# Giving the gathered expert tokens their own contiguous tiles in a two-layer diffusion step with mixture of experts

## The chip, the cores and the metric

The kernel runs on one core of a Trainium2 chip. The metric is the time of one execution on the device in microseconds, as the median of several runs. All weights come from HBM in fp32.

## The reference

Two groups of 128 tokens of width 1024 (a prompt and a sample) go through two layers. Layer 0 is latent attention beside a short convolution, then a dense SwiGLU of inner width 2816. Layer 1 is a convolution module, then a SwiGLU with 8 experts of inner width 3584, of which each token uses the two best. What matters here is the last part:

```python
logits = (t @ router).astype(jnp.float32)
top_v, top_i = lax.top_k(logits, TOP_K)          # TOP_K = 2, t is (256, 1024)
w = jax.nn.softmax(top_v, axis=-1)
gates = jnp.sum(jax.nn.one_hot(top_i, N_EXPERTS) * w[..., None], axis=-2)
for e in range(N_EXPERTS):                       # 8 experts
    out = out + gates[:, e:e + 1] * _swiglu(t, w_gu[e], w_down[e])
```

`_swiglu(h, w_gu, w_down)` is `(silu(h @ gate) * (h @ up)) @ w_down`.

## The kernel before

The program is written engine by engine, each engine with its own fixed list of instructions, and semaphores between them are placed by hand. Nothing derives a wait from the tiles that an instruction touches.

**The weight stream.** SyncE loads weights in pieces of 1 MB into the seven slots of `raw`. ScalarE copies a piece into `high` with the type fp32r (`part` in its `experts`, L763; L489 for the dense pieces), VectorE takes the difference `raw - high` into `low` (L1326), and TensorE multiplies with three products per tile (`mm3`, L1410 to L1412): high half of the tokens by `high`, high half by `low`, low half by `high`. The token tile, 128 x 128, is the stationary operand that is loaded as a weight, and 512 columns of the weight piece are the moving operand. A semaphore `piece_used` then lets SyncE fill the slot again.

**One expert.** Each of the 8 experts has 14 units. A unit is a gate-up product over 8 tiles of the inner dimension (24 matmuls, `gate_up`) into one bank, a Silu on ScalarE (L767), a product on VectorE (L1331), two transposes on TensorE (`e_T`, L1927), a split of the result into `upH` and `upL` (ScalarE L773, VectorE L1336) and a down product of 12 matmuls (`e_down`) that runs two units behind.

**The tokens of an expert.** `gather` (TensorE, L1899) picks up to 128 tokens out of `tokH` and `tokL` by 32 matmuls of 128 columns against `pickR`, in four groups of eight; each group fills one bank and raises `gathered`. `gather_out` (ScalarE, L749 to L755) copies the four banks, one ACTIVATE of 128 x 512 for each, into `slotH` and `slotL` and raises `slot_ready`. `slotH` and `slotL` are no tiles of their own: they are the first 128 of the 256 columns of each of the 8 rows of `hidH` and `hidL`, which hold the split activations of the dense layers and are free by then. `gate_up` reads them as `slotH[:, kk, :]` and `slotL[:, kk, :]`. The profile therefore calls them hidH and hidL.

**Order at the end of an expert.** TensorE transposes the last unit, gathers the tokens of the next expert, does the last two down products of this one, waits for four `slot_ready`, does the first gate-up product of the next expert, and scatters this expert's result (`backR` by `outH` and `outL`, L1969 and L1971). ScalarE does `act_high` of the last unit, the four copies of `gather_out`, three high copies of the weight stream, two copies into `outH` (L802), a further high copy and the next Silu. For expert 0 nothing stands between `gather(0)` and the wait for `slot_ready` but a wait for VectorE's output of a modulation gate (L901). A second pass over all experts is in the program for an expert with more than 128 tokens; it isn't taken here.

**Tiles.** `sb` takes tiles from a stack: those opened with `where=ph` are given back at `ph.close()`, and the next phase begins at the same address. The expert phase begins with `tokH` and `tokL` and goes on with `outH`, `outL`, `eact`, `pick`, `pickR`, `backR` and small tiles.

Of the kernel before, what the change touches and what calls it, by code (L numbers as in the profile page):

```python
# [16 lines left out]
F32R = mybir.dt.float32r  # L17
# [5 lines left out]
P = 128  # L23
D = 1024
KT = D // P
KH = KT // 2
# [105 lines left out]
def ahead(u):  # L132

    return 3 * u + 4 if u else LEAD
# [5 lines left out]
def build(nc, t, outs):  # L140
    ctx = ExitStack()
    with ctx:
        def sb(name, shape, dt=F32, where=None):
            return (where or ctx).enter_context(nc.sbuf_tensor(name, shape, dt))
# [9 lines left out]
        hidH = sb("hidH", [P, KT, TILES * P], F32R)  # L154
        hidL = sb("hidL", [P, KT, TILES * P], F32R)
        gate = sb("gate", [P, TILES, D])
        ph = ExitStack()
# [3 lines left out]
        ph = ExitStack()  # L161
# [14 lines left out]
        ph = ExitStack()  # L176
# [11 lines left out]
        ph = ExitStack()  # L188
        act = sb("act", [P, 2, TILES, UNIT], where=ph)
        ph.close()  # L190
        ph = ExitStack()
# [8 lines left out]
        ph = ExitStack()  # L200
        tokH = sb("tokH", [P, TILES, D], F32R, where=ph)
        tokL = sb("tokL", [P, TILES, D], F32R, where=ph)
        outH = sb("outH", [P, D], F32R, where=ph)
        outL = sb("outL", [P, D], F32R, where=ph)
        eact = sb("eact", [P, 2, UNIT], where=ph)
# [9 lines left out]
        bank = ctx.enter_context(nc.psum_tensor("bank", [P, 8, 512], F32))  # L215
# [11 lines left out]
        prob_l = work[:, HEADS * P:].rearrange("p (h n) -> p h n", h=HEADS)  # L227
        probT = hid[:, 0:4, :].rearrange("p k n -> p (k n)").rearrange("p (g m n) -> p g m n", g=2, m=4)
        rope_t = gate[:, 1, 0:HEADS * ROPE].rearrange("p (h d) -> p h d", h=HEADS)

        slotH, slotL = hidH[:, :, 0:P], hidL[:, :, 0:P]

        sems = {}

        def S(name):
            if name not in sems:
                sems[name] = ctx.enter_context(nc.semaphore(name))
            return sems[name]
# [15 lines left out]
        def cat(ap):  # L254
            return ap.rearrange("p a b -> p (a b)")
# [148 lines left out]
        def expert_value(first, i):  # L404

            slot = (first + i) % RAWS
            within = sum(16 if STREAM_E[m][0] == "d" else 32 for m in range(i + 1) if (first + m) % RAWS == slot)
            per = sum(16 if STREAM_E[m][0] == "d" else 32 for m in range(PER_E) if (first + m) % RAWS == slot)
            passes = (first - N_DENSE) // (EXPERTS * PER_E)
            return slot_total(slot) + passes * EXPERTS * per + within, per  # L410
# [42 lines left out]
        def _(a):  # L453
# [285 lines left out]
            def experts(first, split, passes):  # L739
                ge = passes * EXPERTS  # L740

                def picked(e):

                    a.wait_ge(S("pick_ready"), e + (ge + 1))
                    a.activation(pickR[:, :, :], pick[:, :, :], ACT.Copy).then_inc(S("pickR_ready"), 1)

                def gather_out(e):

                    for part, dst in enumerate((slotH, slotL)):  # L749
                        for kh in range(2):  # L750
                            i = 2 * part + kh
                            a.wait_ge(S("gathered"), e * 4 + (4 * ge + i + 1))
                            a.activation(dst[:, kh * KH:(kh + 1) * KH, :],
                                         bank[:, (6, 0)[part] + kh, :].rearrange("p (k n) -> p k n", k=KH),
                                         ACT.Copy).then_inc(S("slot_ready"), 1)  # L755

                def part(e, kind, u):
                    i = NUM_E[(kind, u)]
                    n, m = first + i, split + i
                    value, per = expert_value(first, i)  # L760
                    a.wait_ge(S(f"raw_in{n % RAWS}"), e * per + value)
                    a.wait_ge(S("piece_used"), e * PER_E + (m - SPLITS + 1))
                    a.activation(high[:, m % SPLITS, :], raw[:, n % RAWS, :], ACT.Copy).then_inc(S("high_ready"), 1)  # L763

                def silu(e, u):
                    a.wait_ge(S("piece_used"), e * PER_E + (split + NUM_E[("b", u)] + 1))
                    a.activation(eact[:, u % 2, :], bank[:, u % 2, 0:UNIT], ACT.Silu).then_inc(S("e_silu"), 1)  # L767

                def act_high(e, w):
                    a.wait_ge(S("e_T"), e * UNITS_E + (ge * UNITS_E + w + 1))  # L770
                    if w >= 2:
                        a.wait_ge(S("piece_used"), e * PER_E + (split + NUM_E[("d", w - 2)] + 1))
                    a.activation(upH[:, w % 2, :, 0:P], bank[:, 2 + w % 2, 0:UNIT].rearrange(  # L773
                        "p (c n) -> p c n", c=UC), ACT.Copy).then_inc(S("e_high"), 1)

                def parts(e, i0, i1, last=True):

                    for i in range(i0, i1):
                        if i < PER_E:
                            part(e, *STREAM_E[i])  # L780
                        elif not last:
                            part(e + 1, *STREAM_E[i - PER_E])

                def body(e, last):
                    for u in range(1, UNITS_E):
                        parts(e, ahead(u - 1), ahead(u), last)
                        silu(e, u)
                        act_high(e, u - 1)
                        if u == 5:
                            a.wait_ge(S("back_T"), e + (ge + 1))  # L790
                            a.activation(cat(backR[:, :, :]), bank[:, 6, 0:TILES * P], ACT.Copy).then_inc(
                                S("back_ready"), 1)
                        if u == 7 and not last:
                            picked(e + 1)
                    parts(e, ahead(UNITS_E - 1), PER_E + 2, last)
                    act_high(e, UNITS_E - 1)
                    if not last:
                        gather_out(e + 1)
                    parts(e, PER_E + 2, PER_E + LEAD - 1, last)
                    for h in range(2):  # L800
                        a.wait_ge(S("piece_used"), e * PER_E + (split + PER_E))
                        a.activation(outH[:, h * 512:(h + 1) * 512], bank[:, 4 + h, :], ACT.Copy).then_inc(  # L802
                            S("out_high"), 1)
                    if not last:
                        parts(e, PER_E + LEAD - 1, PER_E + LEAD, last)
                        silu(e + 1, 0)

                if passes:
                    parts(0, 0, LEAD)
                picked(0)  # L810
                gather_out(0)
                if not passes:
                    parts(0, 3, LEAD)
                silu(0, 0)
                with a.Fori(0, EXPERTS - 1) as e:
                    body(e, False)
                body(EXPERTS - 1, True)
# [1218 lines left out]
```

## Time and profile before

| | |
|---|---|
| median of three runs | 1692.38 us (1691.88 to 1696.34) |
| the profiled execution: its time, its span | 1696.34 us, 1694.6 us |
| instructions | 20850 |
| TensorE matmul busy, weight loads busy | 1532.0 us (90%), 1227.0 us (72%) |
| VectorE, ScalarE, GpSimd busy | 1225.2 us (72%), 975.4 us (58%), 18.6 us (1%) |
| mean granted TensorE clock, in parts of full speed | 0.949 |
| read from HBM | 469.75 MB |

Each engine has its own busy time; a group of instructions is named by the line of the program, the engine, the operation and the tiles, output first. Matmuls are pipelined, so that the duration of one (389 ns) is longer than the distance between the starts of two (0.23 us); the distance is what counts for the time. "PEld" is the loading of stationary operands, which overlaps the matmuls. The experts run from about 682 us to the end.

### The profile page before, as it was taken

To read this page: it belongs to the slowest core of one execution; us is meant where nothing else is said; L and a number is where in the kernel's file an instruction comes from. 1 tells how busy PE (TensorE), PEld (TensorE's weight loads), DVE (VectorE), ACT (ScalarE), POOL (GpSimd) and SP (SyncE) were. 2 spreads that over 40 slices of the span, in tenths; PEclk is the share of its full clock that TensorE was granted. 3 is DMA by queue.
4 is the path that set the end of the run, shared out by engine and by line. 5 is a ranking of instruction groups with operands and counts; after the bars stand their busy time and mean duration, and the time that the engine had idled before them with its cause. 6 is when DMAs were issued, how large, how long until landed. Compare 5 with 4: busy or idle time off the path is not lost.

```text
span 1694.6 us, 20850 instructions
## 1 busy us (share of the span) xinstructions
PE 1532.0 (90%) x7157; PEld 1227.0 (72%) x7157; DVE 1225.2 (72%) x1171; ACT 975.4 (58%) x978; POOL 18.6 (1%) x25
## 2 busy tenths in 40 slices
PE   3658878999788957999999999999999999999996
PEld 1536556888575746788888888888888888888885
DVE  0454555445458744888888988988988988888886
ACT  1231424434244643677777777677677777777773
POOL 0000000000000000000000000000000000000000
PEclk9878899999898978999999999999999999999998
DMA  8455684565535506799999999999999999999993
GB/s 302 171 210 182 213 276 148 188 194 180 173 124 174 199 6 218 241 366 367 326 367 365 331 366 346 354 367 345 353 367 348 353 366 345 355 366 335 353 367 127
DMA packets 340213, 471.64 MB, mean 278 GB/s; under 512 B 13023, under 2 KB 274861, under 8 KB 340158
## 3 DMA queue, kind: packets, MB, share of 16 engines
q1 hardware_dynamic: 336176, 464.43, 80.2%
q0 software_dynamic: 1216, 4.28, 0.7%
q10 hardware_dynamic: 2766, 2.22, 0.4%
q8 instruction: 32, 0.52, 0.1%
q14 instruction: 23, 0.19, 0.0%
HBM read 469.75 MB, written 1.13 MB: 278 GB/s over the span
## 4 chain that ended last, share of the span: by engine, by line
PE 82%; DVE 8%; DMA 3%; ACT 3%; issue 2%; POOL 0%; ACTq 0%; SPq 0%; DVEq 0%; POOLq 0%
PE bank L1410 23%; PE bank L1412 23%; PE bank L1411 23%; PE bank L1785 2%; PE bank L1422 2%; DMA raw<-moe_gu 2%; PE bank L1899 1%; DVE low L833 1%; PE bank L1927 1%; DVE hid L1178 1%; DMA x<-x_sample 1%; PE bank L1439 1%; PE bank L1458 1%; ACT high L489 1%; ACT high L763 1%
## 5 line engine op out<-in xcount | busy, mean ns | idle before, releaser
L1326 DVE TENSOR_TENSOR low<-raw,high 128x2048 fp32r<-128x2048 f32 x333 | 757.4, 2289 | 117.2 <-ACT high L763 109.4
L763 ACT ACTIVATE high<-raw 128x2048 fp32r<-128x2048 f32 x333 | 635.6, 1919 | 182.7 <-DMA raw<-moe_gu 114.0
L1410 PE MATMUL bank<-high,hidH 128*128 128x512 f32 (+1 forms) x1264 | 499.4, 395 | 35.8 <-DVE hidL L870 24.9
L1412 PE MATMUL bank<-high,hidL 128*128 128x512 f32 (+1 forms) x1264 | 495.1, 392 | 0.0
L1411 PE MATMUL bank<-low,hidH 128*128 128x512 f32 (+1 forms) x1264 | 495.1, 392 | 0.0
L1410 PEld LDWEIGHTS bank<-high,hidH 128*128 128x128 f32 x1264 | 239.9, 190 | 91.2 <-DVE hidL L870 28.0
L1412 PEld LDWEIGHTS bank<-high,hidL 128*128 128x128 f32 x1264 | 239.5, 189 | 50.2
L1411 PEld LDWEIGHTS bank<-low,hidH 128*128 128x128 f32 x1264 | 240.1, 190 | 48.9 <-issue 0.2
L1410 PE MATMUL bank<-high,upH 128*128 128x512 f32 (+1 forms) x550 | 227.4, 413 | 2.8 <-DVE upL L963 2.8
L1412 PE MATMUL bank<-high,upL 128*128 128x512 f32 (+1 forms) x550 | 216.9, 394 | 0.0
L1411 PE MATMUL bank<-low,upH 128*128 128x512 f32 (+1 forms) x550 | 215.7, 392 | 0.0
L833 DVE TENSOR_TENSOR low<-raw,high 128x2048 fp32r<-128x2048 f32 (+3 forms) x59 | 131.4, 2245 | 52.3 <-ACT high L489 52.1
L1412 PEld LDWEIGHTS bank<-high,upL 128*128 128x128 f32 x550 | 104.3, 190 | 23.8
L489 ACT ACTIVATE high<-raw 128x2048 fp32r<-128x2048 f32 (+3 forms) x59 | 109.2, 1884 | 18.9 <-DMA raw<-w_in 18.1
L1410 PEld LDWEIGHTS bank<-high,upH 128*128 128x128 f32 x550 | 104.6, 190 | 21.5 <-DVE upL L963 3.0
L1411 PEld LDWEIGHTS bank<-low,upH 128*128 128x128 f32 x550 | 105.0, 191 | 18.5
L767 ACT ACTIVATE eact<-bank 128x256 f32<-128x256 f32 x112 | 42.0, 375 | 61.3 <-PE bank L1412 60.9
L643 ACT ACTIVATE act<-bank 128x256 f32<-128x256 f32 x22 | 7.3, 381 | 109.3 <-PE bank L1412 109.3
L1127 DVE TENSOR_TENSOR act<-act,bank 128x256 f32<-128x256 f32 x22 | 8.3, 418 | 79.6 <-ACT act L643 79.6
L1178 DVE SCALAR_TENSOR_TENSOR hid<-uT,taps,hid 128x256 f32<-128x256 f32 x150 | 60.1, 477 | 0.1
L1422 PE MATMUL bank<-raw,cond 128*32 128x512 f32 x384 | 50.8, 654 | 8.2 <-DVE ada L881 7.8
L697 ACT ACTIVATE diag<-const,taps 128x128 f32<-128x128 f32 x93 | 36.5, 401 | 27.2 <-PE bank L1785 24.9
(222 smaller groups left out, 979.2 us busy)
## 6 DMA issues: line engine op xcount, KB each, us to landing
raw<-moe_gu SPq DMA_DIRECT2D x448, 512.0 KB, 5.4
raw<-moe_down SPq DMA_DIRECT2D x112, 1024.0 KB, 6.3
raw<-ada_w SPq DMA_DIRECT2D x48, 1024.0 KB, 6.1
raw<-ffn_gu SPq DMA_DIRECT2D x44, 512.0 KB, 4.8
raw<-ffn_down SPq DMA_DIRECT2D x11, 1024.0 KB, 4.9
raw<-conv_pw SPq DMA_DIRECT2D x16, 512.0 KB, 4.3
raw<-w_in SPq DMA_DIRECT2D x6, 1024.0 KB, 7.2
raw<-w_o SPq DMA_DIRECT2D x4, 1024.0 KB, 6.9
```

The lines of the kernel that those rows point to most:

```text
L489: a.activation(high[:, n % SPLITS, 0:w], raw[:, m % RAWS, 0:w], ACT.Copy).then_inc(S("high_ready"), 1)
L697: st.mark(a.activation(diag[:, i % DIAGS, :], ident, ACT.Copy, scale=taps[:, j * KT + k:j * KT + k + 1]), "diag_ready")
L763: a.activation(high[:, m % SPLITS, :], raw[:, n % RAWS, :], ACT.Copy).then_inc(S("high_ready"), 1)
L767: a.activation(eact[:, u % 2, :], bank[:, u % 2, 0:UNIT], ACT.Silu).then_inc(S("e_silu"), 1)
L833: v.tensor_tensor(low[:, STREAM[SPLIT[n]] % RAWS, 0:w], raw[:, STREAM[SPLIT[n]] % RAWS, 0:w], high[:, n % SPLITS, 0:w].bitcast(F32), ALU.s ...
L1178: st.mark(v.scalar_tensor_tensor(dst, src, w, dst, ALU.mult, ALU.add), "conv_part")
L1326: v.tensor_tensor(low[:, n % RAWS, :], raw[:, n % RAWS, :], high[:, m % SPLITS, :].bitcast(F32), ALU.subtract).then_inc(S("low_ready"), 1)
L1410: pe.matmul(out, xh, wh, start=start, stop=False)
L1411: pe.matmul(out, xh, wl, start=False, stop=False)
L1412: return pe.matmul(out, xl, wh, start=False, stop=stop)
L1422: last = pe.matmul(bank[32 * k:32 * k + 32, b, :], cond[:, kh * KH + k, :], w_slot(raw, m % RAWS, (KH, 512))[:, k, :], start=kh == 0, stop ...
L1785: st.mark(pe.matmul(bank[:, k % 2, 0:TILES * P].rearrange("p (t n) -> p t n", t=TILES), diag[:, i % DIAGS, :], uT[:, k, :, j:j + P], start ...
```

## The change

`slotH` and `slotL` become tiles of their own, each 128 partitions x 8 x 128 elements (4 KB in a partition), placed in the expert phase between `tokL` and `outH`, so that everything behind them in that phase moves up by 8 KB. The copy in `gather_out` writes 512 consecutive elements and reads a bank of 512 elements as one row, where it had four rows of 128 with a step of 256 elements on the writing side. Waits, semaphores, matmuls, DMAs and the order on each engine stay as they are.

```diff
         tokH = sb("tokH", [P, TILES, D], F32R, where=ph)
         tokL = sb("tokL", [P, TILES, D], F32R, where=ph)
+        slotH = sb("slotH", [P, KT, P], F32R, where=ph)
+        slotL = sb("slotL", [P, KT, P], F32R, where=ph)
         outH = sb("outH", [P, D], F32R, where=ph)
...
-
-        slotH, slotL = hidH[:, :, 0:P], hidL[:, :, 0:P]
...
                             a.wait_ge(S("gathered"), e * 4 + (4 * ge + i + 1))
-                            a.activation(dst[:, kh * KH:(kh + 1) * KH, :],
-                                         bank[:, (6, 0)[part] + kh, :].rearrange("p (k n) -> p k n", k=KH),
+                            a.activation(cat(dst[:, kh * KH:(kh + 1) * KH, :]), bank[:, (6, 0)[part] + kh, :],
                                          ACT.Copy).then_inc(S("slot_ready"), 1)
```

`cat(ap)` is `ap.rearrange("p a b -> p (a b)")`.

## Rows read from the trace of the kernel before

**Rows 1.** The page: its head, and the 40 slices of TensorE, clock and DMA.

```profile
span 1694.6 us, 20850 instructions
PE   3658878999788957999999999999999999999996
PEclk9878899999898978999999999999999999999998
DMA  8455684565535506799999999999999999999993
```

**Rows 2.** Windows of about one expert: span, busy time and count per engine, clock, DMA.

```profile
core 0: us, PE busy (x) PEld busy (x) DVE busy (x) ACT busy (x) POOL busy (x), PEclk, DMA share, GB/s
925.00:1050.00 125.00, 124.39 (x577) 102.49 (x576) 110.19 (x82) 93.03 (x79) 0.00 (x0) 1.00 1.03 354
1175.00:1300.00 125.00, 125.00 (x587) 103.32 (x586) 110.37 (x82) 92.75 (x80) 0.00 (x0) 1.00 1.04 355
```

**Rows 3.** Waits of TensorE's loads, 690 to 1660 us: total, times, longest.

```profile
PEld bank L1927 <- DVE eact L1331: 6.0, 7, 1.7
```

**Rows 4.** DMA from 700 to 1660 us: rates in 40 slices.

```profile
GB/s 364 367 368 375 312 346 366 364 377 315 341 367 368 367 327 346 367 363 367 368 307 366 368 367 368 309 367 363 366 374 300 367 367 368 374 304 343 364 368 373
```

**Rows 5.** Line 753, the copies of `gather_out`: duration min/median/max, first and last start.

```profile
L753 ACT ACTIVATE hidH<-bank x16: 597/597/599, 684.5 to 1550.0; 128x512 fp32r<-128x512 f32 x16
L753 ACT ACTIVATE hidL<-bank x16: 597/597/599, 686.3 to 1551.8; 128x512 fp32r<-128x512 f32 x16
```

**Rows 6.** Groups of ScalarE by shape: copies of 128 x 512 out of a bank.

```profile
L802 ACT ACTIVATE outH<-bank 128x512 fp32r<-128x512 f32 x16 | 8.6, 591 | 5.1 <-PE bank L1412 5.1
L651 ACT ACTIVATE upH<-bank 128x512 fp32r<-128x512 f32 x11 | 6.6, 598 | 3.4 <-PE bank L1704 3.4
L571 ACT ACTIVATE vals<-bank 128x512 f32<-128x512 f32 x3 | 1.7, 579 | 0.0
L618 ACT ACTIVATE hidH<-bank 128x512 fp32r<-128x512 f32 x2 | 1.2, 594 | 0.3 <-PE bank L1642 0.3
```

**Rows 7.** Timeline, end of the first expert, in order of time.

```profile
801.88 0.20 PEld L1927 LDWEIGHTS bank<-const,eact 128*128 128x128 f32 x2 [1.57 <-DVE eact L1331]
803.20 0.60 ACT L753 ACTIVATE hidH<-bank 128x512 fp32r<-128x512 f32 x1 [0.39 <-PE bank L1899]
805.88 0.60 ACT L753 ACTIVATE hidL<-bank 128x512 fp32r<-128x512 f32 x1 [0.30 <-PE bank L1899]
806.37 5.52 ACT L763 ACTIVATE high<-raw 128x2048 fp32r<-128x2048 f32 x3
808.32 6.70 DVE L1326 TENSOR_TENSOR low<-raw,high 128x2048 fp32r<-128x2048 f32 x3 [3.50 <-ACT high L763]
810.98 0.19 PEld L1410 LDWEIGHTS bank<-high,hidH 128*128 128x128 f32 x1
```

**Rows 8.** Timeline, start of the first expert.

```profile
685.77 1.42 DVE L901 TENSOR_TENSOR gate<-bank,gate 128x512 f32<-128x512 f32 x2
687.16 0.60 ACT L753 ACTIVATE hidL<-bank 128x512 fp32r<-128x512 f32 x1 [0.29 <-PE bank L1899]
687.83 0.19 PEld L1410 LDWEIGHTS bank<-high,hidH 128*128 128x128 f32 x1 [0.84 <-DVE gate L901]
```

**Rows 9.** Line 1410, 690 to 1660 us: duration min/median/max, first and last start.

```profile
L1410 PEld LDWEIGHTS bank<-high,hidH x884: 187/188/188, 690.5 to 1659.3; 128*128 128x128 f32 x177
L1410 PEld LDWEIGHTS bank<-high,upH x432: 187/188/192, 704.7 to 1653.9; 128*128 128x128 f32 x144
```

**Rows 10.** The tile hidH from 600 us on: matmuls that read it.

```profile
L1410 PE MATMUL bank<-high,hidH x928: 387/389/796, 625.9 to 1668.0; 128*128 128x512 f32 x186
```

**Rows 11.** Timeline of TensorE: ends of runs of down, gate-up and scatter products.

```profile
806.43 0.39 PE L1410 MATMUL bank<-high,upH 128*128 128x512 f32 x1
...
810.97 0.39 PE L1412 MATMUL bank<-high,upL 128*128 128x512 f32 x1
...
811.88 0.39 PE L1410 MATMUL bank<-high,hidH 128*128 128x512 f32 x1
...
816.41 0.39 PE L1412 MATMUL bank<-high,hidL 128*128 128x512 f32 x1
816.64 0.40 PE L1969 MATMUL bank<-outH,backR 128*128 128x512 f32 x1
818.27 0.39 PE L1971 MATMUL bank<-outL,backR 128*128 128x512 f32 x1
```

## Prediction

> **What bounds the kernel now.** I read the page first, then windows of one expert each, then the waits, and last the stretch around the changed copies. The page shows that TensorE is at nine tenths or more in every slice of the second half, where the experts run, with the clock at its upper level and the DMA engines equally full [rows 1]. The changed instructions run only there. The windows of an expert say the same more sharply: 124.4 and 125.0 us of matmul in 125 us at a granted clock of 1.00, with VectorE at 110 and ScalarE at 93 us [rows 2]. The matmul busy time is modelled, so I checked it by the waits: the loads of TensorE waited for another engine 6.0 us in 970, seven times, all of it for the last activation of an expert, one wait for each boundary between experts [rows 3].
>
> DMA is a close second. It moves 367 GB/s in most slices and falls to 304 to 315 in about one slice in four or five, at the boundaries [rows 4]. One expert needs 3 x 1024 x 3584 x 4 bytes = 44.04 MB, which at 367 GB/s takes 120.0 us. The distance between experts follows from the copies themselves: the first of the first expert starts at 684.5, the second of the eighth at 1550.0 [rows 5], so (1550.0 - 684.5 - 0.9) / 7 = 123.5 us, where 0.9 is the distance from one copy to the next ((805.88 - 803.20) / 3 [rows 7]). TensorE's own list gives that too: 504 matmuls of 512 columns at 0.2265 to 0.227 us (next part) are 114.2 us, and the remaining 9 are the gather, the scatter, the transposes and the wait. So TensorE's list sets the time of the experts, and if it got shorter, DMA would take over 3.5 us further down.
>
> **The copies.** The change touches 4 copies for each of 8 experts, 32 in all. Each takes 597 ns, with hardly a spread (597 to 599) [rows 5]. What would one of 512 consecutive elements take? The nearest rows are the copies of a whole bank of 128 x 512: into `outH`, consecutive and fp32r as the new one will be, 591 ns; into `vals`, 579 ns; into `upH`, a step between parts, 598 ns; and into the first layer's `hidH`, with the very step that the change removes, 594 ns [rows 6]. The stepped ones lie at 594 to 598, the consecutive ones at 579 to 591, so the step costs at most a few ns. I take 591, the row that agrees in type, shape and source, that is 6 ns less. The bounds are 579 (18 ns less) and 598 (1 ns more). In work this is 32 x 6 ns = 0.19 us, at most 0.58 us, of an engine that has about 30 us free in each 125.
>
> The Trainium skill puts a number on such a copy, in "ScalarE: Activation LUTs", section "What ACT_TABLE_LOAD costs": 186 ns and 0.833 ns for each element of a partition, which for 512 is 612 ns whatever the pattern; the rows say 597, and by the page the change would save nothing at all.
>
> **What of it is on the path.** For experts 1 to 7 the copies are paced by the gather: ScalarE stands idle 0.30 to 0.39 us before each, waiting for the next bank, so a shorter copy only makes that idle time longer, and of the four only the last can end earlier. It starts at 805.88 and so ends at 806.48. TensorE needs it for the first load from the gathered tokens, at 810.98 [rows 7]: 4.5 us later, because 24 matmuls of two down products lie between. That cover would have to vanish before 6 ns counted. What stands behind the copies on ScalarE is three high copies, for the first of which VectorE waits 3.50 us [rows 7]. Those would begin 6 ns earlier. But TensorE has no wait for a weight piece in this stretch or elsewhere [rows 3], so this too costs nothing now. SyncE's next loads wait for `piece_used`, which TensorE raises; they do not move.
>
> For expert 0 there is no cover. The profile puts the wait of the first load down to VectorE's gate output, but this ends at 685.77 + 1.42 = 687.19, while the last copy ends at 687.16 + 0.60 = 687.76 and the load starts at 687.83 [rows 8]. The copy is the true releaser, and its 6 ns count once. The sum is 1 x 6 ns, 0.01 us; with all eight last copies on the path and the bound of 18 ns it would be 0.14 us; with the other bound, 0.01 us slower.
>
> **The place of the tiles.** The second part of the change is that 8 x 14 x 24 = 2688 matmuls take their stationary operand from another address; the trace has 928 of the first of three kinds, of which 32 belong to the convolution's output, and (928 - 32) x 3 = 2688 [rows 10]. Each load reads one row of the tile, 128 consecutive elements, before as after: the step of 256 lies between loads and never inside one. The distance between matmuls is (816.41 - 811.88) / 20 = 0.2265 us from `hidH`, and (810.97 - 806.43) / 20 = 0.2270 from `upH`, in another place. The loads themselves are 188 ns in both cases [rows 9, 11] and hidden under the matmul before. I take no change here. The bounds: the scatter, whose stationary operand `backR` is a packed tile of the expert phase, runs at (818.27 - 816.64) / 7 = 0.2329 us [rows 11], which would be 6.4 ns more; and 512 columns at 2.4 GHz are 213.3 ns, 13.2 ns less. The tiles that move up by 8 KB (`outH`, `eact`, `pick`, `backR`) have a few instructions per unit and come under the same verdict. No wait, DMA or instruction is added, and the other use of `hidH` ends before the experts, so freeing it early serves nobody.
>
> **Sum.** Against the profiled execution: 1694.6 us of span - 0.01, and 1.74 us around it, gives 1696.3 us. That execution is the slowest of the three shown; the median is 1692.38, so I forecast 1692.4. The three runs of one kernel lie 4.5 us apart, 0.26%, so 0.3% (5.1 us) is about the least that can be told from no change.
>
> **Rivals.**
> *Slower: the new place makes loads slower.* If stationary operands from a packed tile in this phase made the matmuls follow at the scatter's 0.2329 us, the price is 2688 x 6.4 ns = 17.2 us, all on TensorE's list, 1709.6 us. It decides from 5.1 us / 2688 = 1.9 ns per matmul. For it speaks only that distance; against it, that the scatter has just 8 matmuls behind a change of operands, and that `upH` reads at the distance of `hidH` from elsewhere.
>
> *Faster: the packed tile makes loads faster.* If the step between rows is why matmuls follow at 226.5 ns and not 213.3, 2688 x 13.2 ns = 35.5 us come off TensorE, but DMA holds at 120.0 us an expert, so at most 8 x 3.5 = 28 us are gained: 1664 us. Against it: one load never sees the step.
>
> Of both I also asked whether ScalarE's and VectorE's traffic meets TensorE's reads somewhere that a new address could move. The loads are 187 to 188 ns through 884 of them, while the two engines are busy three quarters and nearly nine tenths of the time [rows 2, 9]; nothing there can be cured or spread. The Trainium skill says the same in "SBUF — State Buffer", section "Who interferes with whom": TensorE and ScalarE wait for nobody at their ports; by that rule, which the trace agrees with, both of these rivals would come out at 1692.4 us.
>
> *Faster: the copies were the stall at the boundaries.* The dips of DMA [rows 4] and VectorE's wait of 3.50 us stand right behind the copies, and a reader could expect that they shrink. If each boundary gained a whole 18 ns for each of its copies, 32 x 18 ns = 0.58 us, 1691.8 us; this remains inside what can be told from no change.
>
> **How the numbers follow.** No change beyond the few ns (with the last rival, which has the same answer at the scale of a measurement): 0.90. The slower rival 0.03, the faster one 0.03. Another 0.02 on each side is for a shift of the median by over 0.3% that comes from the runs' own spread, or from something that no row shows. So faster 0.05, same 0.90, slower 0.05. The range must hold the run spread (1691.88 to 1696.34) and a part of the slower bound: a median near the slowest run is 1696.3. Below, 0.58 us of copies and a little of the run spread, on the side on which no run lies: 1689.5. Above I add 0.7 us for 0.26 ns per matmul of the placement: 1697.0. The two large rivals lie outside, with 0.10 in all.
>
> **What would show it.** In the new trace the copies should be called slotH and slotL and take 579 to 598 ns, likeliest 591, each still after about 0.3 us of idle time. The experts should remain 123.5 us apart, matmuls from slotH 0.2265 us apart, their loads 188 ns, and VectorE's wait at the boundary about 3.5 us. The prediction is wrong if the distance of those matmuls moves by 2 ns or more, if TensorE shows new waits at a boundary, or if a stretch before 682 us, which runs the same list, changes.

## The result, and the profile after

The changed kernel takes 1710.62 us (median of 6 runs, 1709.50 to 1712.48) against 1695.45 us (6 runs, 1691.88 to 1701.28): ratio 1.0089, 95% interval 1.0072 to 1.0105, 15 us slower. I had forecast 1692.4 with a range to 1697.0. The page of the kernel after, head and slices:

```profile
span 1712.2 us, 20850 instructions
PE   3658878999788957999999999999999999999996
PEclk9778799999898977999999999999999999999998
DMA  8455584665535505799999999999999999999993
```

The program has as many instructions as before, and the picture is that of [rows 1]. One expert's windows, columns as in [rows 2]:

```profile
925.00:1050.00 125.00, 125.00 (x571) 101.63 (x570) 108.36 (x81) 91.32 (x78) 0.00 (x0) 1.00 1.02 350
1175.00:1300.00 125.00, 125.00 (x572) 101.62 (x570) 108.17 (x82) 90.60 (x77) 0.00 (x0) 1.00 1.02 349
```

TensorE is still full and its clock still 1.00, but the trace has 571 and 572 matmuls in 125 us where it had 577 and 587. It also waits less. All waits of its loads from 690 to 1660 us, to be read beside the 6.0 us of [rows 3]:

```profile
PEld bank L1409 <- DVE gate L900: 0.8, 1, 0.8
```

So in the experts work, clock and waits don't explain the loss; what is left is the distance between matmuls. The timeline of TensorE at the place of [rows 11], the end of the first expert (fourth and last of 24 gate-up matmuls, then the first and last of the scatter):

```profile
817.24 0.40 PE L1409 MATMUL bank<-high,slotH 128*128 128x512 f32 x1
...
821.92 0.40 PE L1411 MATMUL bank<-high,slotL 128*128 128x512 f32 x1
822.16 0.39 PE L1968 MATMUL bank<-outH,backR 128*128 128x512 f32 x1
...
823.76 0.39 PE L1970 MATMUL bank<-outL,backR 128*128 128x512 f32 x1
```

From the tokens it is (821.92 - 817.24) / 20 = 0.2340 us, where it was 0.2265. The scatter went from 0.2329 to (823.76 - 822.16) / 7 = 0.2286. The loads have not changed, and neither have the down products of the same kernel. Line 1410, 690 to 1680 us, duration min/median/max:

```profile
L1410 PEld LDWEIGHTS bank<-low,slotH x888: 187/188/192, 692.3 to 1677.2; 128*128 128x128 f32 x178
L1410 PE MATMUL bank<-low,slotH x888: 392/397/400, 692.6 to 1677.4; 128*128 128x512 f32 x178
L1410 PE MATMUL bank<-low,upH x435: 387/389/396, 709.9 to 1679.7; 128*128 128x512 f32 x145
```

The matmuls from the new tiles have 397 ns, those from `upH` 389. Over all neighbouring pairs of gate-up matmuls from 700 to 1660 us, some 2500 in each trace, the mean distance is 227.6 ns before and 234.6 after.

The copies, line 753, and their place at the end of the first expert:

```profile
L753 ACT ACTIVATE slotH<-bank x16: 598/600/600, 688.9 to 1565.6; 128x512 fp32r<-128x512 f32 x16
L753 ACT ACTIVATE slotL<-bank x16: 597/600/600, 690.7 to 1567.4; 128x512 fp32r<-128x512 f32 x16
```

```profile
811.20 0.60 ACT L753 ACTIVATE slotL<-bank 128x512 fp32r<-128x512 f32 x1 [0.29 <-PE bank L1898]
813.63 6.70 DVE L1325 TENSOR_TENSOR low<-raw,high 128x2048 fp32r<-128x2048 f32 x3 [2.91 <-ACT high L762]
816.54 0.39 PE L1409 MATMUL bank<-high,slotH 128*128 128x512 f32 x1
```

They take 600 ns, 3 more than the rows of four, and the last of them ends at 811.80, 4.7 us before TensorE's first matmul from it.

**Where the 15 us are.** The experts lie (1565.6 - 688.9 - 0.9) / 7 = 125.1 us apart, 1.6 more than before, 12.8 us for eight. The sum agrees: 2688 x 7.0 ns = 18.8 us more on TensorE's list, less the 6.0 us of waits that went away (a slower TensorE no longer catches up with the stream), is 12.8 us. The first copy came 4.4 us later, at 688.9 instead of 684.5, in a part of the program that did not change. There the granted clock makes the difference, as the stretch from 0 to 200 us shows, first before, then after:

```profile
0.00:200.00 200.00, 126.22 (x673) 92.65 (x677) 79.16 (x127) 52.69 (x93) 11.52 (x14) 0.82 0.60 211
```

```profile
0.00:200.00 200.00, 126.41 (x641) 92.45 (x643) 75.86 (x120) 51.52 (x91) 11.54 (x14) 0.80 0.60 211
```

With 0.82 granted there were 673 matmuls behind it after 200 us, with 0.80 only 641. This varies from execution to execution: in the fourteen traces of this study the first copy came at 679.2 to 683.4 us where 0.85 was granted in these 200 us, at 684.1 to 684.8 with 0.82 and at 688.1 to 688.9 with 0.80, in kernels with and without the change alike (one experiment, moving_128b, stands apart and is explained there). The runs of the kernel before lay up to 1.2% apart. So the 12.8 us in the experts are the change's; the two traces, whose spans lie 17.6 us apart, and the two medians, 15.2 us, hold a share of this spread as well. I therefore read each experiment by two numbers that it doesn't touch, the distance of matmuls and the distance of experts, and by the time second.

### The profile page after: what moved, and what is told of

It is laid out like the page before. It is cut to its first block, busy times and chain, and to the rows that moved or that the text cites. A ratio compares the mean times of both kernels' runs of the same rounds, so it can differ in the third digit from the quotient of the medians.

```text
span 1712.2 us, 20850 instructions
## 1 busy us (share of the span) xinstructions
PE 1552.9 (91%) x7157; PEld 1232.0 (72%) x7157; DVE 1226.0 (72%) x1171; ACT 975.4 (57%) x978; POOL 18.6 (1%) x25
## 4 chain that ended last, share of the span: by engine, by line
PE 86%; DVE 8%; ACT 2%; DMA 1%; issue 1%; POOL 0%; ACTq 0%; DVEq 0%; POOLq 0%
PE bank L1409 24%; PE bank L1411 24%; PE bank L1410 24%; PE bank L1784 2%; PE bank L1421 2%; PE bank L1898 1%; DVE low L832 1%; PE bank L1926 1%; DVE hid L1177 1%; PE bank L1438 1%; DMA x<-x_sample 1%; PE bank L1457 1%; ACT high L489 1%; DVE hidL L869 1%; DMA gate<-ada_b 1%
## 5 line engine op out<-in xcount | busy, mean ns | idle before, releaser
L1409 PE MATMUL bank<-high,slotH 128*128 128x512 f32 x896 | 356.2, 398 | 0.7 <-DVE gate L900 0.7
L1411 PE MATMUL bank<-high,slotL 128*128 128x512 f32 x896 | 355.5, 397 | 0.0
L1410 PE MATMUL bank<-low,slotH 128*128 128x512 f32 x896 | 355.0, 396 | 0.0
L1411 PEld LDWEIGHTS bank<-high,slotL 128*128 128x128 f32 x896 | 168.6, 188 | 40.8
L1409 PEld LDWEIGHTS bank<-high,slotH 128*128 128x128 f32 x896 | 168.7, 188 | 40.6 <-DVE gate L900 0.8
L1410 PEld LDWEIGHTS bank<-low,slotH 128*128 128x128 f32 x896 | 168.8, 188 | 39.9
L1409 PE MATMUL bank<-high,hidH 128*128 128x512 f32 (+1 forms) x368 | 149.0, 405 | 35.2 <-DVE hidL L869 25.0
L1410 PE MATMUL bank<-low,hidH 128*128 128x512 f32 (+1 forms) x368 | 146.6, 398 | 0.0
L1411 PE MATMUL bank<-high,hidL 128*128 128x512 f32 (+1 forms) x368 | 146.1, 397 | 0.0
L1409 PEld LDWEIGHTS bank<-high,hidH 128*128 128x128 f32 x368 | 71.8, 195 | 56.0 <-DVE hidL L869 28.0
```

Source lines behind the costliest of these rows:

```text
L1409: pe.matmul(out, xh, wh, start=start, stop=False)
L1410: pe.matmul(out, xh, wl, start=False, stop=False)
L1411: return pe.matmul(out, xl, wh, start=False, stop=stop)
```

## The experiments

I needed the addresses, which the profile doesn't show. They follow from the sizes in order of declaration once the first is known; that one, 16512, is read from the compiled program and stands in no trace. In each partition `low` starts at 16512, `high` at 73856, `hidH` at 139392, `upH` at 163968. All four are 128 past a multiple of 1024. The phase of the experts begins behind small tiles: `slotH` got 199648, 992 past a multiple of 1024, 32 past a multiple of 64. The difference of two tiles does not hang on the first address: `slotH` lies 199648 - 73856 = 125792 bytes behind `high`, that is 491 x 256 + 96.

Beside the experiments the kernel before had a median of 1701 us on each of three chips, 6 us more than the 1695.45 of its six runs above, and the ratios of the experiments are against that. Against 1701 the 1710.62 us of the changed kernel would be 1.006: in time the change costs 0.6 to 0.9%, and the 12.8 us of the experts, 0.75%, lie between.

The four new facts of the changed kernel are then: the rows start at another place within 64 bytes (theory 1), they lie 512 and not 1024 bytes apart (theory 2), and the tiles lie in another region and shift what is behind them (theory 3); the fourth is the flat copy. One kernel for each.

**own_aligned**

```diff
+        sb("pad0", [P, 8], where=ph)
         slotH = sb("slotH", [P, KT, P], F32R, where=ph)
         slotL = sb("slotL", [P, KT, P], F32R, where=ph)
+        sb("pad1", [P, 8], where=ph)
```

> The changed kernel with 32 bytes per partition of unused space before slotH and 32 after slotL, so that both tiles start at a multiple of 1024 bytes instead of 32 past a multiple of 64. Theory 1 (the start of a stationary row within 64 bytes sets the distance of the matmuls): distance back at 226.7 ns, time as before, ratio 0.997 to 1.003. Theory 2 (rows 512 bytes apart instead of 1024) and theory 3 (the region of the expert phase): nothing changes against the changed kernel, mean distance about 234 ns, ratio 1.007 to 1.011.

Measured: 1705.01 us, ratio 1.002 (0.9989 to 1.005). The rows of TensorE's timeline that answer to the ones above, fourth and last of 24:

```profile
811.46 0.39 PE L1411 MATMUL bank<-high,slotH 128*128 128x512 f32 x1
...
816.11 0.39 PE L1413 MATMUL bank<-high,slotL 128*128 128x512 f32 x1
```

(816.11 - 811.46) / 20 = 0.2325 us, mean 233.2 ns, experts 124.7 us apart. The time alone can't be told from no change and would speak for theory 1; the distance says that the matmuls are still slow. Theory 1 missed. (The experts are 8 x 1.2 = 9.6 us longer and the median only 3.7 us; that the spread ahead of the experts hides the rest is likely but not shown.)

**own_rows_apart**

```diff
-        slotH = sb("slotH", [P, KT, P], F32R, where=ph)
-        slotL = sb("slotL", [P, KT, P], F32R, where=ph)
+        slots = sb("slots", [P, KT, 2, P], F32R, where=ph)
+        slotH, slotL = slots[:, :, 0, :], slots[:, :, 1, :]
```

The copies are those of the kernel before, four rows with a step.

> The new tiles in the same 8 KB of the expert phase, but the rows of slotH and slotL in turn, so that the rows of each lie 1024 bytes apart as in the kernel before; every row still starts 32 bytes past a multiple of 64. Theory 2 (step): distance 226.7 ns, ratio about 1.000. Theory 1 (start) and theory 3 (region): distance about 234 ns, ratio 1.007 to 1.011.

Measured: 1712.60 us, ratio 1.0056 (1.0026 to 1.0087), mean distance 234.6 ns, experts 125.1 us apart: distance and experts as in the changed kernel, and the time too (1710.62 us; its ratio of 1.0089 was against the faster six runs). Neither the step nor the form of the copy plays a part.

**old_place_packed**

```diff
-        slotH, slotL = hidH[:, :, 0:P], hidL[:, :, 0:P]
+        slotH = hidH[:, :, :].rearrange("p k n -> p (k n)")[:, 0:KT * P].rearrange("p (k n) -> p k n", k=KT)
+        slotL = hidL[:, :, :].rearrange("p k n -> p (k n)")[:, 0:KT * P].rearrange("p (k n) -> p k n", k=KT)
```

(with the flat copy of the change)

> No new tiles: slotH and slotL are the first 1024 consecutive elements of hidH and hidL, rows 512 bytes apart, starts at a multiple of 64, copies in one row. Theory 2 (step): about 234 ns, ratio 1.007 to 1.011. Theory 1 (start) and theory 3 (region): 226.7 ns, ratio about 1.000.

Measured: 1700.86 us, ratio 0.9984 (0.9962 to 1.0006).

```profile
811.38 0.39 PE L1409 MATMUL bank<-high,hidH 128*128 128x512 f32 x1
...
815.91 0.39 PE L1411 MATMUL bank<-high,hidL 128*128 128x512 f32 x1
```

(815.91 - 811.38) / 20 = 0.2265 us, mean 227.6. The packed form and the flat copy, which is all that the change has beside the new place, cost nothing and gain nothing.

**old_place_32b**

```diff
-        slotH, slotL = hidH[:, :, 0:P], hidL[:, :, 0:P]
+        slotH, slotL = hidH[:, :, 8:P + 8], hidL[:, :, 8:P + 8]
```

> The kernel before with the slots at columns 8 to 135 of each row of hidH and hidL instead of 0 to 127: the same place, step and copies, but every row starts 32 bytes past a multiple of 64. Theory 1 (start): about 234 ns, ratio 1.007 to 1.011, with no other part of the change made. Theory 2 (step) and theory 3 (region): 226.7 ns, ratio about 1.000.

Measured: 1707.09 us, ratio 1.0036 (1.001 to 1.0063), experts 124.8 us apart.

```profile
812.32 0.40 PE L1410 MATMUL bank<-high,hidH 128*128 128x512 f32 x1
...
816.99 0.40 PE L1412 MATMUL bank<-high,hidL 128*128 128x512 f32 x1
```

(816.99 - 812.32) / 20 = 0.2335 us. Thirty-two bytes in the old place are enough for almost the whole loss per matmul, so theory 3 isn't needed, but own_aligned says that a multiple of 64, even of 1024, is not the good place either. The good place so far was 128 past a multiple of 1024 or of 512, which is where `high` and `low` start too. That gave theory 4: the start counts within a few hundred bytes, either against the start of the moving operand (4a) or in itself (4b).

**own_like_high**: as own_aligned, with `pad0` of 40 elements (160 bytes) instead of 8.

> The changed kernel with 160 bytes per partition of unused space before slotH and 32 after slotL, so that slotH and slotL start at 128 past a multiple of 1024 bytes, which is where high, low, hidH and upH start too. Theory 3 (the region of the expert phase, or what moved up with it): still about 233 to 234 ns, ratio 1.003 to 1.010. Theory 4 (what counts is the start of the stationary row, within 512 bytes, and the place of hidH happens to be the right one): distance 226.7 ns after ten matmuls, experts 123.5 us apart, ratio 0.997 to 1.003.

Measured: 1703.25 us, ratio 1.0006 (0.9979 to 1.0033), experts 123.7 us apart.

```profile
815.94 0.39 PE L1411 MATMUL bank<-high,slotH 128*128 128x512 f32 x1
...
820.47 0.40 PE L1413 MATMUL bank<-high,slotL 128*128 128x512 f32 x1
```

(820.47 - 815.94) / 20 = 0.2265 us. The tiles of the change, in their own region and packed, are as fast as the old ones once they are moved by 160 bytes. Theory 3 falls.

**all_128b**: the kernel before, with 128 bytes ahead of everything.

```diff
+        sb("pad_all", [P, 32])
         ring = ExitStack()
         raw = sb("raw", [P, RAWS, PIECE], where=ring)
```

> The kernel before with 128 unused bytes per partition ahead of every tile: all tiles start 128 bytes further, stationary and moving operands alike, at 256 past a multiple of 1024. Theory 4a (the start of the stationary row in relation to the start of the moving operand counts): 226.7 ns, ratio about 1.000. Theory 4b (the stationary row's own start within 512 bytes must be 128): about 233 ns in the experts and in the dense layers alike, ratio 1.005 to 1.015. Theory 3 (region): 226.7 ns.

Measured: 1692.56 us, ratio 0.9953 (0.9928 to 0.9978), mean distance 227.6 ns, experts 122.9 us apart. Rows now start at 256 past a multiple of 1024, as do the moving operands, and the matmuls are fast: the rule is one of two operands, 4a. That the kernel got faster was not expected; I come back to it.

**old_place_128b** and **old_place_256b**: as old_place_32b, with columns from 32 and from 64.

> The kernel before with the slots at columns 32 to 159 of each row of hidH and hidL: rows start at 256 past a multiple of 1024, moving operands stay at 128. Theory 4a and 4b: slow, 229 to 235 ns. Theory 1 in its old form (only the place within 64 bytes counts) and theory 3: 226.7 ns.

> The kernel before with the slots at columns 64 to 191 of each row of hidH and hidL: rows start at 384 past a multiple of 1024. Theory 4a and 4b: slow if the period is 512 bytes, 226.7 ns if it is 128 or 256 bytes, in which case the slow own_aligned was slow by its region (theory 3).

Measured, one execution each, so without a ratio: 1710.61 us, mean distance 233.2 ns, experts 124.7 us apart; and 1694.37 us, 227.6 ns, 123.5 us. Rows at 256 past a multiple of 1024 are slow while `high` is at 128, and fast in all_128b, where `high` is at 256 too. And 256 bytes away from `high` is as good as none.

**moving_128b**: all_128b with 128 more bytes behind `high`, so that all tiles but `low` and `high` move by another 128.

```diff
         high = sb("high", [P, SPLITS, PIECE], F32R)
+        sb("pad_high", [P, 32])
```

> The kernel before with 128 unused bytes ahead of all tiles and 128 more behind high: low and high start 128 bytes further (256 past a multiple of 1024) and all other tiles 256 bytes further, which puts stationary and moving operands 128 bytes apart within 256 everywhere, though the stationary tiles start at 384, where columns 64 to 191 of hidH were fast. Theory 4a with a period of 256 bytes (start of the stationary row against start of the moving row): both gate-up and down matmuls, dense and expert, at about 233 ns on average; 4032 + dense matmuls slow, ratio 1.008 to 1.02 less what the DMAs gain. Theory 4b (the stationary row's own start): 226.7 ns, ratio as all_128b, about 0.995. The DMA rate in the experts tells whether all_128b gained by the start of raw at a multiple of 256: then 372 GB/s here too, not 367.

Measured: 1715.01 us, ratio 1.0078 (1.0052 to 1.0105).

```profile
823.35 0.39 PE L1412 MATMUL bank<-high,hidH 128*128 128x512 f32 x1
...
827.99 0.40 PE L1414 MATMUL bank<-high,hidL 128*128 128x512 f32 x1
```

(827.99 - 823.35) / 20 = 0.2320 us, mean 233.2, and here the down products from `upH` are slower too (those with `low` 231.1 ns on average, 228.4 before), and the first copy comes at 695.2 us, because the dense layers pay as well: from 300 to 430 us the matmuls that read `high` and `low` follow at 232.4 ns, in the other thirteen traces at 227.0. 1.0078 / 0.9953 puts the price of 128 bytes between the two operands, in dense layers and experts alike, at 1.3% of the kernel. The DMA rate in its full slices was not 372 GB/s but 362 to 369; the changed kernel, as slow and with `raw` in the old place, has 358 to 368 there. A slower TensorE presumably asks for no more, so the rate could not tell what I wanted of it.

**old_place_64b**

> The kernel before with the slots at columns 16 to 143 of each row of hidH and hidL, 64 bytes away from the moving operand's start. Theory 4a with a period of 256 bytes: slow, 229 to 236 ns on average. If the period were 64 bytes with another reason for the slow 128, 226.7 ns.

Measured, one execution: 1706.94 us, mean 233.9 ns, experts 124.7 us apart.

**all_256** and **own_all_256**: the kernel before, and the changed one, both with

```diff
+        sb("pad_all", [P, 32])
         ring = ExitStack()
...
+        sb("pad_tok", [P, 40], where=ph)
         tokH = sb("tokH", [P, TILES, D], F32R, where=ph)
```

> The kernel before with 128 unused bytes ahead of all tiles and 160 ahead of tokH: every large tile, those of the expert phase too, starts at a multiple of 256 bytes. Theory 4a: 226.7 ns in steady state as in all_128b; if the ten slow matmuls after each pair of transposes come from the transposes' own operands (eact against the identity, 96 bytes apart within 256 before), they shorten and an expert takes 1 us less than in all_128b; if they come from the interruption itself, nothing moves. Time against before: 0.993 to 0.997.

> The changed kernel with the same two paddings as all_256, so that slotH and slotL start at a multiple of 256 bytes as low and high do. Theory 4a: the same time as all_256 within 0.2%, 226.7 ns; the change in itself then is worth nothing. Theory 3 (something in the region or in the copies costs): slower than all_256 by 0.3% or more.

Measured: 1689.08 us, ratio 0.9927 (0.9903 to 0.9951), and 1691.66 us, ratio 0.9935 (0.9911 to 0.9958), experts 122.6 us apart in both. Their medians are 0.15% apart, inside both intervals: the change in itself is worth nothing that can be measured, and both of these beat the kernel before and the kernel after. The gate-up matmuls and the scatter of all_256:

```profile
805.57 0.39 PE L1412 MATMUL bank<-high,hidH 128*128 128x512 f32 x1
...
810.11 0.39 PE L1414 MATMUL bank<-high,hidL 128*128 128x512 f32 x1
```

(810.11 - 805.57) / 20 = 0.2270 us, and the eight matmuls of the scatter, 0.2329 before, now follow at 226.7 ns on average.

**All fourteen in one table.** "Away" is the start of a stationary row less the start of the moving operand, modulo 256 bytes; the distance is the mean over neighbouring gate-up matmuls from 700 to 1660 us.

| kernel | away, bytes | distance, ns | experts apart, us | time against before |
|---|---|---|---|---|
| before | 0 | 227.6 | 123.5 | |
| after | 96 | 234.6 | 125.1 | 1.0089 |
| own_aligned | 128 | 233.2 | 124.7 | 1.002 |
| own_rows_apart | 96 | 234.6 | 125.1 | 1.0056 |
| old_place_packed | 0 | 227.6 | 123.8 | 0.9984 |
| old_place_32b | 32 | 233.6 | 124.8 | 1.0036 |
| own_like_high | 0 | 227.6 | 123.7 | 1.0006 |
| all_128b | 0 | 227.6 | 122.9 | 0.9953 |
| old_place_128b | 128 | 233.2 | 124.7 | |
| old_place_256b | 0 | 227.6 | 123.5 | |
| moving_128b | 128 | 233.2 | 124.9 | 1.0078 |
| old_place_64b | 64 | 233.9 | 124.7 | |
| all_256 | 0 | 227.3 | 122.6 | 0.9927 |
| own_all_256 | 0 | 227.4 | 122.6 | 0.9935 |

The distance and the experts are from one trace of each kernel; the ratio of the kernel after is against other runs than those below it, as said above. The seven kernels with 0 have 227.3 to 227.6, the seven with 32 to 128 have 233.2 to 234.6, with nothing between, and equal values give equal distances (96 twice, in the same region; 0 seven times and 128 three times, in the old region and in the new). That the period is 256 bytes and not more rests on old_place_256b; no difference between 128 and 256 was tried.

## Why the prediction was wrong

**The failed step** is "The place of the tiles", where I wrote "I take no change here" for 2688 matmuls. It was mis-sized: 0 ns taken, 7.0 ns measured, 18.8 us of TensorE's time. The changed kernel puts the rows of the tokens 96 bytes (modulo 256) away from the start of the weight pieces, where `hidH` lay 0 away. This is shown by own_like_high, which keeps all of the change and moves its tiles by 160 bytes, and by old_place_32b, which makes none of the change and moves the slots by 32.

**Why the row misled me.** I argued from `upH` "in another place", which ran like `hidH`. It was another address, but not another place in the sense that counts: `upH` also starts 128 past a multiple of 1024, as everything up to `const` does, since each tile before it is a multiple of 1024 bytes. All rows at 0.2265 came from one and the same case. The only row that differed, the scatter at 0.2329, I held for a transient behind a change of operands.

**The rival.** The slower rival had the right matmuls, the right sign, a price of 6.4 ns (7.0 measured) and a time of 1709.6 us (1710.62). I gave it 0.03. Its condition, a packed tile in this phase, was wrong: old_place_packed is packed and fast, own_like_high is packed, in this phase, and fast. Its size was luck too: the scatter's two operands lie 0 apart modulo 256, and in all_256, where the whole phase agrees with the weight pieces, it runs at 226.7 ns. So its 0.2329 was indeed a transient, as I held against it; such transients are described in the last section. The price also isn't what reached the end: the rival left out that waits of 6.0 us would go.

The faster rival, that the step between rows is why matmuls follow at 226.5, is refuted by old_place_packed (227.6 with and without the step). The rule of the Trainium skill that I set beside both ("SBUF — State Buffer", section "Who interferes with whom", that TensorE waits for nobody at its ports) would have had no change at all. The runs show 15 us. The rule speaks of one engine waiting for another, and the loads, which kept their 188 ns, agree with it. I had read it as if no address could matter for the distance of TensorE's own matmuls, and there the measurement decides.

**The copies.** Forecast 591 ns, measured 600, 9 ns off and over the bound of 598. In old_place_packed and own_like_high the same flat copy takes 597, and in own_rows_apart the old form at the new place takes 600: so the flat form is worth nothing, and the 3 ns go with the place. What of the place it is stays open: old_place_32b, also 32 bytes past a multiple of 64, has 598, and so has own_aligned at a multiple of 1024. That none of it reaches the end is right: the copies still stand behind 0.29 us of idle time, and the last ends 4.7 us before it is needed (4.5 forecast). For expert 0 the copy is again the last to end, 691.56 + 0.60 = 692.16, 0.07 us before the load. VectorE's wait at the end of the first expert is 2.91 us (3.50 before).

**What bounds the kernel.** That TensorE's list sets the pace held: 7.0 ns on each of 2688 matmuls came out at the end, less only the waits. The dips of DMA that I gave as 304 to 315 GB/s "in about one slice in four or five" were misread: [rows 4] has seven in 40 slices, one for each boundary, from 300 to 327. Nothing in the sum hung on that. "DMA would take over 3.5 us further down" used 367 GB/s as a ceiling; in all_256 most slices run at 370 to 377, so it was one for that place of `raw` at most.

**The range** rested on runs of one kernel; the bound of +17.2 us was worked out and then left outside it because of the 0.03. Of the signs of being wrong that I had named, the first came true: the distance moved by 7.0 ns, where 2 were the mark. New waits at a boundary didn't come. The stretch before 682 us did change, by 4.4 us, but that goes with the granted clock and not with the change.

## What to carry to other kernels

When a tile that TensorE loads as stationary moves, compare its start with that of the moving operand modulo 256 bytes, and pad so that they agree; here, with fp32r operands, 32 to 128 bytes of difference cost 6 to 7 ns on every matmul of 512 columns, which is about 3% of TensorE's rate and showed in no wait and in no load. Before a row of "another place" is taken as evidence, look whether its address differs in the bits that could matter. And where the run-to-run spread is as large as the effect, judge an experiment by the distance between instructions in its own trace: own_aligned looked cured by its time and was not by its distance.

## What the runs showed of the hardware

**Two operands and 256 bytes.** At 0 bytes away the distance settles at 226.7 ns for matmuls of 512 fp32r columns at a granted clock of 1.00. At 96 it goes through a pattern of seven distances (231 to 237 ns on average) and does not come down in 24 matmuls, at 128 through another of seven (228 to 241 in own_aligned, 230 to 237 in moving_128b), and at 64 it ends in turns of 230.8 and 235.8. What inside the chip does this was not measured.

**It takes some matmuls to settle.** In the kernel before, the nine distances that follow the first one after a pair of transposes average between 224 and 236 ns, and from then on it is 226.7. Together these nine are some 46 ns longer than nine settled ones. In all_256, where the transposes' operand `eact` starts at a multiple of 256 as the identity does (96 away before), it is five, between 228 and 236, together 25 ns longer. With some 15 such interruptions in an expert this is 0.3 us, and the experts moved from 122.9 us apart in all_128b to 122.6. That it was `eact` and no other tile of that phase was not separated.

**DMAs into aligned slots take less time.** The unexpected gain of all_128b goes with this: the slots of `raw` start at a multiple of 256 bytes (with the 16512 above), 128 past one before. The queue of the weight loads from 700 to 1660 us (packets, MB, time of its packets as a share of 16 engines), before, then all_128b, then moving_128b:

```profile
q1 hardware_dynamic: 257797, 341.01, 103.9%
```

```profile
q1 hardware_dynamic: 256555, 340.41, 99.9%
```

```profile
q1 hardware_dynamic: 254925, 336.02, 99.7%
```

Per MB that is 0.305, 0.293 and 0.297%. The changed kernel, which moves 336.49 MB in the same time as moving_128b, has 102.0%, 0.303. Over all traces the ten with `raw` in the old place have 0.303 to 0.306, the four with 128 bytes ahead of it 0.293 to 0.297. So the packets take 2 to 4% less time in these four, and the rate in most slices of all_128b is 370 to 376 GB/s instead of 367. TensorE's 6.0 us of waits at the boundaries are gone there, and 8 x (123.5 - 122.9) = 5 us is what the experts gained, of some 8 us in the medians; where the others come from was not looked into. That the start of `raw` and not another tile that moved with it does this was not tried alone, since `raw` and `low` share their bytes.
